# Window-state keys and values loaded from all 128 position blocks: another cut of the state rows into DMA transfers

## The chip, the cores and the metric

The kernel runs on one core of a Trainium2 chip. The metric is the device time of one execution in microseconds; the time of the kernel before is the median of three runs. Views of the profile come from one profiled execution, whose own time stands beside the median below.

## The reference, cut to what matters

One inference step of a decoder layer for 512 prompt tokens and 8 samples with 8 new tokens each. Two attentions run per layer. The change is in the second one for the samples: each new token looks at the last 2048 positions of its sample (the window state, 2048 rows of 8 heads x 64 = 2 KB for keys and as much for values) with three dilations.

```
DIL_PAIRS = ((128, 1), (512, 4), (2048, 16))
def _dilated_attention_sample(q, k_new, v_new, k_buf, v_buf):
    w = k_buf.shape[1]                                  # 2048
    k_all = jnp.concatenate([k_buf, k_new], axis=1)
    v_all = jnp.concatenate([v_buf, v_new], axis=1)
    for window, d in DIL_PAIRS:
        n_k = window // d + 1
        idx = (w + jnp.arange(t))[:, None] - d * jnp.arange(n_k)[None, :]
        kg, vg = k_all[:, idx], v_all[:, idx]
        sc = jnp.einsum('bthd,btjhd->bthj', q, kg) * SCALE
        ...
        parts.append((einsum(e, vg), m, sum(e)))
    o = _combine_branches(parts)
```

The eight new tokens need, of each block of 16 positions, the positions 0 to 7 of all 128 blocks (dilation 16), and the positions 8 to 15 of the last 32 blocks only (dilations 4 and 1). That is 1280 of the 2048 positions.

## The kernel before

The state is viewed as `sk` and `sv`, [sample, p, i, 512]: 128 blocks p, 16 positions i, and 512 floats (2 KB) for a position. So a position lies 2 KB behind the one before it, and a block 32 KB behind the block before it.

Work on past keys and values runs in slots. A slot handles one group q of 512 positions for each of two samples ("pages" of 128 positions, four to a group and sample). Groups q = 0 to 31 come from the paged cache (items 0 to 3, L102 `QUADS`), groups 32 to 43 from the state: items 4 to 7, each two samples, each three groups. The first two groups g = 0, 1 of an item are 64 blocks x positions 0 to 7 (four pages); the third is 32 blocks x positions 8 to 15 (two pages). Keys of group q are handled in slot t = q, its values eight slots later (`LAG`), so the values of the state are used in slots 40 to 51, and from slot 44 (`KSLOTS`) on there are no keys left to do.

Keys: SyncE loads two pages in one DMA into `k_ring` (L832, 512 KB, source made by `state_pair`); VectorE turns them into `kt_sb` (L2271), TensorE scores them (L1296), VectorE adds the mask `lw` and keeps them in `s_sb` (L2308), ScalarE takes the exponentials (L1826). The mask is a host constant that says how often position `keys` is looked at (L79, L81), so it follows whatever order the loads give the positions.

Values: `place_state` (L708) issues eight DMAs a group. For the first two groups each is one quarter of the blocks, 16 blocks x positions 0 to 7: 16 runs of 16 KB at the source, written as 128 rows of 2 KB. For a third group a DMA takes 8 blocks x 8 positions to 64 rows, 128 KB. GpSimd issues those of slots 40 to 43 (all into `v_ring`), SyncE those of slots 44 to 46 and the first halves of 47 to 51, ScalarE the second halves of 47 to 51 between its own work (L1800); after slot 43 the freed `k_ring` and `kt_sb` (as `t_ring`) serve as buffers beside `v_ring`. TensorE turns the probabilities (L1309), ScalarE copies them into `pt_sb` (L1791, for third groups L1795), and TensorE multiplies values by them: L1333 for halves of a group, L1350 for a whole third group. A load into a ring waits until the matmuls of its former content are done (`pv_half`). The order of all this is written out by hand as the sequence of slots t and steps i of each engine's program.

Cache pages (L697, `place_page`) take another form: a page of 128 positions goes to 32 rows of `v_ring`, every fourth, in four pieces of 2 KB a row, so that it is 32 x 4 pieces.

Behind slot 51 the samples' output projection (L1372) and the feed-forward part follow, which need all of it.

Of the kernel before, what the change touches and what calls it, by code (L numbers as in the profile page):

```python
# [15 lines left out]
P = 128  # L16
# [40 lines left out]
def constants():  # L57

    c = np.zeros((P, C_END), np.float32)
    pos = np.concatenate([np.arange(SEQ), PAST + np.arange(NS) % DT]).astype(np.float32)  # L60
    inv = (10000.0 ** (-np.arange(32) / 32)).astype(np.float32)
    ang = (pos[:, None] * inv[None, :]).astype(np.float32).T
    for q in range(4):
        c[32 * q:32 * q + 32, C_COS:C_COS + NT] = np.cos(ang)
        c[32 * q:32 * q + 32, C_SIN:C_SIN + NT] = np.sin(ang) * (1 if q % 2 else -1)
    dist = (SEQ - P) + np.arange(P)[:, None] - np.arange(SEQ)[None, :]
    c[:, C_WMASK:C_WMASK + SEQ] = log_count(dist)
    c[:, C_DMASK:C_DMASK + SEQ] = np.where(dist >= 0, 0, NEG)
    c[:, C_ID:C_ID + P] = np.eye(P)

    p = np.arange(P)
    t, second, b = p % DT, p // 16 % 2, p // DT % 4
    for g in range(3):
        n = 4 if g < 2 else 2
        j, x = np.arange(32 * n) // n, np.arange(32 * n) % n
        if g < 2:
            keys = 16 * (64 * g + 16 * b[:, None] + j // 2) + 4 * (j % 2) + x  # L79
        else:  # L80
            keys = 16 * (96 + 8 * b[:, None] + j // 4) + 8 + 2 * (j % 4) + x  # L81
        c[:, C_LW + P * g:C_LW + P * g + 32 * n] = log_count(WBUF + t[:, None] - keys)
    same = t[:, None] == np.arange(32)[None, :] % DT
    c[:, C_SEL:C_SEL + 32] = same
    c[:, C_SEL + 32:C_SEL + 64] = np.where(same, 0, NEG)

    col = np.arange(MINI_W) - (NS - 2 * DT)
    own = (col[None, :] // DT == second[:, None]) & (col[None, :] >= 0)
    new = t[:, None] - col[None, :] % DT
    c[:, C_MINI:C_MINI + MINI_W] = np.where(own & (new >= 0), 0, NEG)  # L90
    c[:, C_MINI + MINI_W:C_MINI + 2 * MINI_W] = np.where(own, log_count(new), NEG)
    c[:, C_FLAGS] = p % 16 >= DT
    c[:, C_FLAGS + 1] = second == 0
    c[:, C_FLAGS + 2] = second == 1
    c[:, C_FLAGS + 3] = p < 64
    c[:, C_FLAGS + 4] = p >= 64
    return c
# [19 lines left out]
def pages_of(q):  # L117
    it, g = item_of(q)
    return 2 if it >= 4 and g == 2 else 4
# [184 lines left out]
def key_load(q, i):  # L304


    return i | 1 if q >= FIRST[4] else i
# [16 lines left out]
def landings():  # L324


    seen, k_lands, v_lands = [[0] * 8 for sems in range(4)], {}, {}
    for q in range(KSLOTS):
        for i in range(8):
            if i % 4 < pages_of(q):  # L330
                seen[0][i] += key_load(q, i) == i
                k_lands[q, i] = 16 * seen[0][i]
    for q in range(KSLOTS):
        for h in range(2):
            for i in value_loads(q, h):
                s = value_sem(q, i)
                here = seen[sems_of(q + LAG)]
                here[s] += 1
                v_lands[q, s] = 16 * here[s]
    return k_lands, v_lands  # L340
# [56 lines left out]
def build(nc, ins, outs):  # L397
    from contextlib import ExitStack
    ctx = ExitStack()
    with ctx:  # L400
# [299 lines left out]
        def state_rows(state, q, b):  # L700


            it, g = item_of(q)
            if pages_of(q) == 4:
                return state[2 * (it - 4) + b, 64 * g:64 * g + 64, 0:8, :]
            return state[2 * (it - 4) + b, 96:P, 8:16, :]

        def place_state(queue, q, h):  # L708


            ring = ring_of(q + LAG)
            for i in value_loads(q, h):
                s, b = divmod(i, 4)
                rows = slice(0, P) if pages_of(q) == 4 else slice(64 * s, 64 * s + 64)
                src = state_rows(sv, q, s).rearrange("(b a) i c -> b a i c", b=4)[b]
                dst = (k_ring[rows, 4 * h + b, :], v_ring[rows, h, b, :], t_ring[rows, h, b, :])[ring]
                queue.dma_start(dst, src).then_inc(
                    (k_landed, v_landed, t_landed, p_landed)[sems_of(q + LAG)][value_sem(q, i)], 16)
# [23 lines left out]

            return n * 8 + (16 - 8 * par)

        def state_pair(state, q, i):


            n, k = pages_of(q), i % 4
            return state_rows(state, q, i // 4).rearrange("p (s x) c -> p s x c", x=n)[:, :, k - 1:k + 1, :]

        @block.sync
        def _(sp):
# [70 lines left out]
            def load_keys(t, i):  # L823

                if has_k(t) and i % 4 < pages_of(t) and key_load(t, i) == i:
                    if t:
                        last, h = t - 1, i // 4
                        sp.wait_ge(kt_done, PAGE_NO[last, i] + 1 if i % 4 < pages_of(last) else half_end(last, h))
                    if t < FIRST[4]:
                        load_keys_page(t, i)  # L830
                    else:
                        sp.dma_start(k_ring[:, i - 1:i + 1, :], state_pair(sk, t, i)).then_inc(k_landed[i], 16)  # L832

            first_ids = {}

# [1926 lines left out]
```

## Time and profile before

| | |
|---|---|
| median of 3 runs | 1072.36 us (1069.6 to 1074.74) |
| profiled execution, its own time | 1075.88 us |
| its span | 1074.2 us |
| TensorE matmuls busy | 951.3 us, 89% |
| VectorE, ScalarE, GpSimd busy | 667.1, 517.2, 289.1 us |
| DMA | 310.99 MB, mean 290 GB/s |

The span starts 1.7 us short of the execution's own time. TensorE is the busiest engine over the whole, but its share is not even: the part from about 566 to 662 us, where values of the state are used and the prompt's work runs out, is the one with gaps. A view by stretches shows for each the busy time of the engines, the granted TensorE clock as a share of the full one, the share of time in which the DMA engines held packets (two packets in flight make it go slightly over 1) and the GB/s that they moved.

### The profile page before, as it was taken

What the parts mean: (1) busy time and instruction counts of PE and PEld (TensorE: products, weight loads), DVE (VectorE), ACT (ScalarE), POOL (GpSimd) and SP (SyncE); (2) the same over time, 40 slices, a digit from 0 to 9 for tenths busy, and PEclk for the clock granted to TensorE, in tenths of its full rate; (3) what the DMA queues carried; (4) which work ended last, traced back from release to release, by engine and by line L of the source; (5) the groups of instructions that cost most, each with busy time, mean ns of one, the idle gap of its engine ahead of it and who ended that gap; (6) DMA issues with size and microseconds to landing.
All of it is one profiled execution on the core that took longest, in us unless ns stands there. A gap on an engine that the chain in (4) does not pass through costs nothing.

```text
span 1074.2 us, 29350 instructions
## 1 busy us (share of the span) xinstructions
PE 951.3 (89%) x11042; PEld 846.5 (79%) x11042; DVE 667.1 (62%) x1632; ACT 517.2 (48%) x1128; POOL 289.1 (27%) x351
## 2 busy tenths in 40 slices
PE   3989899899977789898996567899999999999996
PEld 3978788788855567676775444899999999999996
DVE  5279745676469978863564254888888888700004
ACT  6554533375226559664332652554555555611114
POOL 1321154545533355335553000000000000133331
PEclk8999999899989989999999688999999999999998
DMA  8799999999999999889998995578687786975642
GB/s 239 256 306 342 328 326 377 355 370 369 382 368 363 355 369 344 303 312 385 378 280 225 239 222 155 209 258 328 235 310 273 266 319 227 336 246 170 219 149 88
DMA packets 158165, 310.99 MB, mean 290 GB/s; under 512 B 13985, under 2 KB 88098, under 8 KB 157026
## 3 DMA queue, kind: packets, MB, share of 16 engines
q1 hardware_dynamic: 133922, 233.92, 63.0%
q0 software_dynamic: 22400, 72.37, 19.2%
q10 hardware_dynamic: 1728, 3.15, 1.2%
q8 instruction: 74, 1.21, 0.5%
q14 instruction: 41, 0.34, 0.1%
HBM read 302.31 MB, written 73.92 MB: 350 GB/s over the span
## 4 chain that ended last, share of the span: by engine, by line
PE 37%; issue 31%; DMA 15%; DVE 7%; ACT 4%; POOL 2%; SPq 2%; POOLq 1%; ACTq 0%; DVEq 0%
PE ps L1468 11%; PE ps L1102 8%; DMA v_ring<-in_cache_v_diff 8%; PE ps L1333 4%; DMA v_ring<-in_state_v_win 4%; PE ps L1296 4%; DMA k_ring<-in_cache_k_diff 3%; DVE kt_sb L2271 2%; PE ps L1253 2%; PE ps L1179 1%; DVE prob L2163 1%; PE ps L1350 1%; PE ps L1163 1%; PE ps L1148 1%; POOL v_ring L697 1%
## 5 line engine op out<-in xcount | busy, mean ns | idle before, releaser
L2271 DVE STREAM_TRANSPOSE kt_sb<-k_ring 128x512 f32<-128x512 f32 x336 | 219.5, 689 | 73.3 <-DMA k_ring<-in_cache_k_diff 35.5
L697 POOL DMA_DIRECT2D v_ring<-in_cache_v_diff x248 | 136.8, 553 | 154.6 <-issue 83.8
L1041 POOL TENSOR_TENSOR c_lo<-c_raw,c_hi 128x1408 fp32r<-128x1408 f32 x14 | 46.7, 3337 | 416.1 <-ACT c_hi L1884 416.1
L1102 PE MATMUL ps<-h_hi,w_hi 128*128 128x288 f32 x384 | 124.2, 323 | 1.9 <-DVE h_lo L2125 1.9
L1102 PE MATMUL ps<-h_lo,w_hi 128*128 128x288 f32 x384 | 115.1, 300 | 0.0
L1102 PE MATMUL ps<-h_hi,w_lo 128*128 128x288 f32 x384 | 114.8, 299 | 0.0
L1333 PE MATMUL ps<-v_ring,pt_sb 128*32 128x128 f32 x2240 | 80.5, 286 | 33.5 <-DMA v_ring<-in_cache_v_diff 21.6
L1296 PE MATMUL ps<-kt_sb,q_st 128*32 128x128 f32 (+1 forms) x2816 | 95.0, 277 | 6.9 <-DVE q_st L2281 4.1
L997 POOL TENSOR_TENSOR w_lo<-w_raw,w_hi 128x1024 fp32r<-128x1024 f32 x24 | 57.3, 2388 | 152.0 <-ACT w_hi L1585 152.0
L1333 PEld LDWEIGHTS ps<-v_ring,pt_sb 128*32 128x32 f32 x2240 | 62.6, 114 | 45.2 <-issue 41.6
L1296 PEld LDWEIGHTS ps<-kt_sb,q_st 128*32 128x32 f32 x2816 | 71.6, 112 | 24.0 <-issue 17.1
L1102 PEld LDWEIGHTS ps<-h_hi,w_hi 128*128 128x128 f32 x384 | 74.0, 193 | 15.7 <-issue 13.5
L1468 PE MATMUL ps<-a_hi,c_hi 128*128 128x288 f32 x352 | 79.1, 296 | 0.2 <-POOL c_lo L1041 0.2
L1401 PE MATMUL ps<-t_h,s_h 128*128 128x288 f32 x264 | 77.9, 295 | 1.2 <-ACT u L1877 1.2
L1468 PE MATMUL ps<-a_lo,c_hi 128*128 128x288 f32 x352 | 78.9, 295 | 0.0
L1468 PE MATMUL ps<-a_hi,c_lo 128*128 128x288 f32 x352 | 78.5, 294 | 0.0
L1401 PE MATMUL ps<-t_l,s_h 128*128 128x288 f32 x264 | 77.9, 295 | 0.0
L1401 PE MATMUL ps<-t_h,s_l 128*128 128x288 f32 x264 | 77.7, 294 | 0.0
L2410 DVE TENSOR_TENSOR s_l<-s_t,s_h 128x512 fp32r<-128x512 f32 x88 | 58.8, 689 | 28.4 <-ACT s_h L1848 18.1
L1102 PEld LDWEIGHTS ps<-h_lo,w_hi 128*128 128x128 f32 x384 | 74.2, 193 | 0.0
L1102 PEld LDWEIGHTS ps<-h_hi,w_lo 128*128 128x128 f32 x384 | 74.0, 193 | 0.0
L2561 DVE TENSOR_TENSOR x<-x,ps 128x512 f32 x7 | 4.8, 689 | 111.1 <-PE ps L1481 111.1
(248 smaller groups left out, 2354.2 us busy)
## 6 DMA issues: line engine op xcount, KB each, us to landing
k_ring<-in_cache_k_diff SPq DMA_DIRECT2D x256, 256.0 KB, 6.8
v_ring<-in_cache_v_diff POOLq DMA_DIRECT2D x248, 256.0 KB, 6.7
out_k_win_sample<-in_state_k_win SPq DMA_DIRECT2D x32, 1020.0 KB, 8.3
out_v_win_sample<-in_state_v_win SPq DMA_DIRECT2D x32, 1020.0 KB, 8.0
k_ring<-in_state_k_win SPq DMA_DIRECT2D x40, 512.0 KB, 7.0
w_raw<-in_w_in SPq DMA_DIRECT2D x24, 512.0 KB, 7.5
g_raw<-in_w_gate SPq DMA_DIRECT2D x11, 1024.0 KB, 5.3
g_raw<-in_w_up SPq DMA_DIRECT2D x11, 1024.0 KB, 5.4
```

The source lines that it names most:

```text
L697: queue.dma_start(dst, src.rearrange("(b j) c -> j b c", b=4))\
L997: nc.gpsimd.tensor_tensor(w_lo[:, n % 3, :], w_raw[:, n % 3, :], w_hi[:, n % 2, :].bitcast(F32), ALU.subtract).then_inc(w_lo_done, 1)
L1041: nc.gpsimd.tensor_tensor(c_lo[j][:, 0:width], c_raw[:, j, 0:width], c_hi[j][:, 0:width].bitcast(F32), ALU.subtract).then_inc(w_lo_done, 1)
L1102: last = nc.tensor.matmul(M[c][:, 0:HALF], wt, act[:, k, c * HALF:(c + 1) * HALF], start=k == 0 and at_first, stop=k == KT - 1 and act is ...
L1148: last = nc.tensor.matmul(M[c][:, 0:n], qT[r, T, qb * P:(qb + 1) * P], kT[r, T, 0:n], start=True, stop=True)
L1253: last = nc.tensor.matmul(M[m % 2], wt, act[:, k, :], start=k == 0 and at_first, stop=k == KT - 1 and act is mix_h and not at_first)
L1296: last = nc.tensor.matmul(S[32 * f:32 * f + 32, c0:c0 + 32 * n], q_st[place_of(it)][:, h, f, r, :], kt_sb[:, 4 * h:4 * h + n, c:c + 32], s ...
L1333: last = nc.tensor.matmul(O[32 * f:32 * f + 32, P * h:P * h + P], pt_sb[:, 4 * f + b, :], values[:, f * P:(f + 1) * P], start=g == 0 and b ...
L1401: last = nc.tensor.matmul(ps[:, bank, 0:HALF], wt[:, k, :], act[:, k, :], start=j in (0, 1, 3) and k == 0 and at_first, stop=k == 3 and wt ...
L1468: last = nc.tensor.matmul(main_ps[:, 2 * bank + c, 0:HALF], wt[j][:, w], a_lo[:, pair, block, :] if low else a_hi[pair][:, block, :], star ...
L2271: V.transpose(kt_sb[:, i, :], k_ring[:, i, :]).then_inc(kt_done, 1)
L2410: V.tensor_tensor(dst[:, :, :], src, high[:, :, :].bitcast(F32), ALU.subtract).then_inc(form_low, 1)
```

## The change

The same positions are read, cut in another way, and the mask constants follow.

```
@@ constants
         if g < 2:
-            keys = 16 * (64 * g + 16 * b[:, None] + j // 2) + 4 * (j % 2) + x
+            keys = 16 * (32 * b[:, None] + j) + 4 * g + x
         else:
-            keys = 16 * (96 + 8 * b[:, None] + j // 4) + 8 + 2 * (j % 4) + x
+            keys = 16 * (96 + 16 * (b[:, None] % 2) + j // 2) + 8 + 4 * (b[:, None] // 2) + 2 * (j % 2) + x
@@ state_rows
             if pages_of(q) == 4:
-                return state[2 * (it - 4) + b, 64 * g:64 * g + 64, 0:8, :]
+                return state[2 * (it - 4) + b, :, 4 * g:4 * g + 4, :]
             return state[2 * (it - 4) + b, 96:P, 8:16, :]
@@ place_state
                 s, b = divmod(i, 4)
-                rows = slice(0, P) if pages_of(q) == 4 else slice(64 * s, 64 * s + 64)
-                src = state_rows(sv, q, s).rearrange("(b a) i c -> b a i c", b=4)[b]
+                if pages_of(q) == 4:
+                    place_page(queue, q, i, state_rows(sv, q, s)[:, b, :])
+                    continue
+                rows = slice(64 * s, 64 * s + 64)
+                src = state_rows(sv, q, s).rearrange("(r a) (u i) c -> u r a i c", r=2, u=2)[b // 2, b % 2]
@@ keys
-        def state_pair(state, q, i):
-            n, k = pages_of(q), i % 4
-            return state_rows(state, q, i // 4).rearrange("p (s x) c -> p s x c", x=n)[:, :, k - 1:k + 1, :]
+        def place_pair(queue, q, i):
+            rows, k = state_rows(sk, q, i // 4), i % 4
+            if pages_of(q) == 4:
+                queue.dma_start(k_ring[:, i - 1:i + 1, :], rows[:, k - 1:k + 1, :]).then_inc(k_landed[i], 16)
+            else:
+                for u in range(2):
+                    src = rows[:, 4 * u:4 * u + 4, :].rearrange("p (s x) c -> p s x c", x=2)
+                    queue.dma_start(k_ring[64 * u:64 * u + 64, i - 1:i + 1, :], src).then_inc(k_landed[i], 16)
```

So a first or second group is now positions 4g to 4g + 3 of all 128 blocks. A DMA of its values is one position of all 128 blocks (256 KB as 128 separate pieces of 2 KB, 32 KB apart at the source), written by `place_page` as a cache page is. A DMA of its keys is two neighbouring positions of 128 blocks (128 pieces of 4 KB). A third group's values go as 16 blocks x 4 positions to a DMA (16 runs of 8 KB), and its keys in two DMAs of half the size instead of one; `landings` counts two arrivals for them.

The instructions of TensorE, VectorE, ScalarE and GpSimd keep kind, number and order; the shapes of the value loads change. In GpSimd's program, at the values of slots 40 to 43, before:

```order
L1018 TENSOR_TENSOR o_lo<-wo_sb,o_hi_64 128x1024
L717 DMA v_ring<-in_state_v_win 128x1x512 x4
L717 DMA v_ring<-in_state_v_win 64x1x512 x8
L717 DMA v_ring<-in_state_v_win 128x1x512 x8
L1068 UNCONDITIONAL_BRANCH
```

and with the change:

```order
L1027 TENSOR_TENSOR o_lo<-wo_sb,o_hi_64 128x1024
L698 DMA v_ring<-in_state_v_win 32x4x512 x4
L721 DMA v_ring<-in_state_v_win 64x1x512 x8
L698 DMA v_ring<-in_state_v_win 32x4x512 x8
L1077 UNCONDITIONAL_BRANCH
```

Nothing moved; the destination of a first or second group's load is 32 rows of four pieces instead of 128 rows of one. In SyncE's program, from the last state keys (one item's third group and all later ones) to the loads behind the last values, before:

```order
L910 DMA g_ffn<-in_norm_ffn_g 128x1024
L832 DMA k_ring<-in_state_k_win 128x1x1024 x16
L717 DMA k_ring<-in_state_v_win 128x1x512 x4
L717 DMA t_ring<-in_state_v_win 128x1x512 x4
L717 DMA k_ring<-in_state_v_win 128x1x512 x4
L717 DMA v_ring<-in_state_v_win 64x1x512 x8
L717 DMA t_ring<-in_state_v_win 128x1x512 x4
L717 DMA k_ring<-in_state_v_win 128x1x512 x4
L803 DMA g_raw<-in_w_gate 128x8x256
L717 DMA v_ring<-in_state_v_win 64x1x512 x8
```

and with the change:

```order
L919 DMA g_ffn<-in_norm_ffn_g 128x1024
L754 DMA k_ring<-in_state_k_win 128x1024 x4
L758 DMA k_ring<-in_state_k_win 64x1x1024 x4
L754 DMA k_ring<-in_state_k_win 128x1024 x8
L758 DMA k_ring<-in_state_k_win 64x1x1024 x4
L698 DMA k_ring<-in_state_v_win 32x4x512 x4
L698 DMA t_ring<-in_state_v_win 32x4x512 x4
L698 DMA k_ring<-in_state_v_win 32x4x512 x4
L721 DMA v_ring<-in_state_v_win 64x1x512 x8
L698 DMA t_ring<-in_state_v_win 32x4x512 x4
L698 DMA k_ring<-in_state_v_win 32x4x512 x4
L812 DMA g_raw<-in_w_gate 128x8x256
L721 DMA v_ring<-in_state_v_win 64x1x512 x8
```

The 16 key loads became 20; the order is the same, and the third groups' value loads keep the destination of 64 rows.

## Rows read from the trace of the kernel before

**Rows 1.** Stretches: us, busy us of the engines (xinstructions), clock, DMA share, GB/s.
```profile
541.00:566.00 25.00, 24.90 (x362) 19.05 (x358) 15.69 (x48) 9.62 (x29) 13.14 (x18) 1.00 0.93 274
566.00:580.00 14.00, 10.25 (x128) 7.49 (x120) 6.46 (x17) 1.79 (x7) 4.49 (x8) 0.88 0.91 223
580.00:618.00 38.00, 21.50 (x408) 17.36 (x408) 11.88 (x54) 20.29 (x45) 4.21 (x8) 0.71 0.99 234
618.00:662.00 44.00, 29.64 (x496) 20.98 (x491) 22.16 (x47) 19.53 (x35) 0.00 (x0) 0.86 0.79 207
662.00:1074.20 412.20, 396.74 (x2969) 391.29 (x2969) 250.28 (x393) 185.03 (x315) 46.71 (x14) 0.99 0.65 239
```

**Rows 2.** Short stretches in which one kind of transfer ran; columns as in rows 1.
```profile
500.00:528.00 28.00, 26.98 (x350) 20.32 (x344) 11.96 (x40) 6.95 (x18) 16.06 (x20) 0.94 1.03 395
552.20:553.80 1.60, 1.60 (x36) 1.13 (x34) 0.71 (x2) 0.70 (x1) 0.00 (x0) 1.00 1.02 392
545.00:550.00 5.00, 5.00 (x57) 3.81 (x51) 3.71 (x9) 0.41 (x3) 4.38 (x5) 1.00 1.00 268
597.00:605.50 8.50, 5.30 (x80) 4.38 (x84) 2.30 (x8) 7.84 (x17) 0.00 (x0) 0.50 1.06 260
571.00:575.00 4.00, 3.96 (x40) 3.11 (x41) 2.61 (x4) 0.00 (x0) 0.01 (x1) 0.66 1.05 193
608.00:612.00 4.00, 1.09 (x8) 0.86 (x8) 1.01 (x6) 3.95 (x12) 0.00 (x0) 1.00 1.07 165
652.50:656.50 4.00, 1.45 (x34) 1.04 (x34) 2.21 (x4) 0.84 (x2) 0.00 (x0) 1.00 0.55 196
```

**Rows 3.** TensorE in order of time: start us, us, work, [idle before <- releaser].
```profile
571.04 1.08 PE L1333 MATMUL ps<-v_ring,pt_sb 128*32 128x128 f32 x32 [2.25 <-DMA v_ring<-in_state_v_win]
...
580.41 2.01 PE L1350 MATMUL ps<-v_ring,pt_sb 128*32 128x128 f32 x64 [1.91 <-DMA v_ring<-in_state_v_win]
...
591.63 1.93 PE L1333 MATMUL ps<-v_ring,pt_sb 128*32 128x128 f32 x32 [5.34 <-DMA v_ring<-in_state_v_win]
...
614.56 3.67 PE L1350 MATMUL ps<-v_ring,pt_sb 128*32 128x128 f32 x64 [5.22 <-DMA v_ring<-in_state_v_win]
...
650.46 1.08 PE L1333 MATMUL ps<-k_ring,pt_sb 128*32 128x128 f32 x32 [1.15 <-DMA k_ring<-in_state_v_win]
653.12 1.08 PE L1333 MATMUL ps<-k_ring,pt_sb 128*32 128x128 f32 x32 [1.57 <-DMA k_ring<-in_state_v_win]
...
657.19 3.33 PE L1350 MATMUL ps<-v_ring,pt_sb 128*32 128x128 f32 x64 [2.62 <-DMA v_ring<-in_state_v_win]
```

**Rows 4.** ScalarE in order of time; the copies of third groups' probabilities.
```profile
578.54 0.84 ACT L1795 ACTIVATE pt_sb<-ps,mini_mask 128x256 f32<-128x256 f32 x2 [12.21 <-PE ps L1309]
...
610.28 0.47 ACT L1795 ACTIVATE pt_sb<-ps,mini_mask 128x256 f32<-128x256 f32 x1
...
654.60 0.84 ACT L1795 ACTIVATE pt_sb<-ps,mini_mask 128x256 f32<-128x256 f32 x2 [2.83 <-PE ps L1309]
```

**Rows 5.** Issues of value loads by GpSimd and SyncE, in order of time.
```profile
566.51 4.49 POOL L717 DMA_DIRECT2D v_ring<-in_state_v_win  x8 [5.65 <-PE ps L1333]
583.01 4.21 POOL L717 DMA_DIRECT2D v_ring<-in_state_v_win  x8 [12.01 <-PE ps L1350]
...
593.62 5.92 SPq L717 DMA_DIRECT2D v_ring<-in_state_v_win  x8
...
641.15 5.11 SPq L717 DMA_DIRECT2D v_ring<-in_state_v_win  x8
```

**Rows 6.** All state value transfers: us from issue to landing.
```profile
DMA to landing us min/median/max: 3.6/8.8/18.5
```

**Rows 7.** State key loads: issue ns min/median/max; SyncE's wait before them, 530 to 664 us.
```profile
L832 SPq DMA_DIRECT2D k_ring<-in_state_k_win x40: 534/535/649, 420.9 to 572.5; - x40
...
SPq L832 <- DVE kt_sb L2271: 39.3, 9, 8.9
```

More of the change, by code:

```diff
@@ L330, in landings @@
             if i % 4 < pages_of(q):
-                seen[0][i] += key_load(q, i) == i
+                if key_load(q, i) == i:
+                    seen[0][i] += 1 if pages_of(q) == 4 else 2
                 k_lands[q, i] = 16 * seen[0][i]
@@ L831, in load_keys @@
                     else:
-                        sp.dma_start(k_ring[:, i - 1:i + 1, :], state_pair(sk, t, i)).then_inc(k_landed[i], 16)
+                        place_pair(sp, t, i)
             first_ids = {}
```

## The prediction

> **What bounds the kernel now.** I read the stretches first [rows 1]. To 566 us TensorE is busy 24.90 of 25.00 us: a faster load gives nothing there. From 662 us on it is busy 396.74 of 412.20 us with work that the change does not touch. Between lie 96 us in which it is busy 10.25 + 21.50 + 29.64 = 61.4 us at a granted clock of 0.88, 0.71 and 0.86, while the DMA engines held packets for 0.91, 0.99 and 0.79 of the time and yet moved only 223, 234 and 207 GB/s. The slots 40 to 51, whose values come from the state, run there. So the gain or loss must be made in 566 to 662 us, and the rate of these loads is the question.
>
> Then the rate by kind of transfer [rows 2], from stretches in which only one kind ran. Cache pages and state keys together: 395 GB/s. State keys alone: 392. State values of first and second groups: 268 issued by GpSimd, 260 by SyncE, the engines full both times. Third groups: 193 with full engines (GpSimd's), 165 where they share the queue with others (SyncE's, from 608), and 196 at a DMA share of 0.55 (from 652.5), which is half of the engines working at full rate and the rest with nothing. The pieces of values have 2 KB on the side of the buffers, as a cache page's have, and the buffers are the same. What is left as a cause is where the pieces lie at the source, and for third groups how many engines get a share.
>
> Last, what this costs on the path: the waits of TensorE for values [rows 3]. They are 2.25, 1.91, 5.34, 5.22, 1.15, 1.57 and 2.62 us, 20.1 in all; an eighth, 2.65 us before 597.64, is not shown, since it lies in the shadow of ScalarE (below).
>
> **First and second groups' values.** 64 DMAs of 256 KB change form, 48 of them issued after 580 us. Number, bytes, order and issuing engines stay. The new source is 128 pieces of 2 KB at a distance of 32 KB, and no trace of before shows just that. Bounds: the slowest row for values of the state, 165 GB/s, and the fastest with pieces of any form, 392 to 395 [rows 2]. I take the upper end, by the row of state keys, which is nearest: they too are 128 separate pieces, come from rows 32 KB apart with the same offsets within the 32 KB for all engines at once, and still ran at 392. The values of before differ from them in that an engine walks one run of 16 KB while its neighbours walk the runs 32 KB beside it, and this form is the slow one.
>
> **Third groups' values.** 32 DMAs of 128 KB: 8 blocks x 8 positions become 16 blocks x 4 positions. The share of 0.55 [rows 2] says that 8 of 16 engines carried SyncE's. With 16 blocks all sixteen have a share. Bounds: still 193 GB/s (all engines full, as GpSimd's at 571) to 392; in between lies 260, since 16 runs beside each other is the form of today's first groups. A group's values are 1.05 MB, thus 2.7 to 5.4 us. More important is that the queue is no longer uneven: the loads behind a third group no longer wait on half the engines.
>
> The Trainium skill says the same of the cause in "DMA: Bandwidth & Descriptors", section "Why a DMA increments its semaphore by 16 and not by 1": the number of engines is the largest up to 16 that divides the slowest dimension of both sides, so 8 for 8 blocks and 16 for 16. The trace agrees with its 0.55. By it the third groups alone would improve, and the rest of the change would be indifferent, which is the first rival's time.
>
> **The path, step by step** (rows 3 to 6; least time from a value load's issue to its landing 3.6 us [rows 6]).
> - Before 582 us: the wait of 2.25 us goes. The next, 1.91 us, was for a third group issued from 566.51 to 571.00 [rows 5]; at 3.6 to 5.4 us it lands by 576.5. ScalarE's copy that L1350 also needs ended at 579.38 [rows 4], so of the 580.41 about 1.0 us is to be had. Together 3.3 us.
> - 591.63: GpSimd starts these loads when L1350 is done, 583.01 [rows 5]. Four issues are half of 4.21, so 585.1, plus 3.6 is 588.7 against 591.5: 2.8 us. The following half's wait (2.65 us) gives nothing more, since ScalarE is busy 7.84 of 8.50 us from 597 on [rows 2] and is next late.
> - 614.56: the loads are issued from 593.62 to 599.54 [rows 5]; they would land by 605 at the latest. ScalarE's copy of the probabilities ends at 610.75 [rows 4], so L1350 starts about 610.9: 3.7 us.
> - 618 to 646: no wait for values; ScalarE, VectorE and TensorE hand each other work. 0.
> - 650.46 and 653.12: 1.15 + 1.57 = 2.7 us. 657.19: the copy ends at 655.44 [rows 4], L1350 at 655.6: 1.6 us. The loads for it, issued 641.15 to 646.26 [rows 5], land by 650.
>
> Sum 3.3 + 2.8 + 3.7 + 2.7 + 1.6 = 14.1 us. From 580 to 657 us some 18 MB of loads pass (48 x 0.26 + 3 x 1.05 + 2.1 of weights); at 392 GB/s that is 46 us, well inside the shortened stretch. I take 13, because a shift passes between engines with an order of their own and not one to one. What is late next is ScalarE.
>
> **Keys.** First and second groups: 32 DMAs of 128 pieces of 4 KB as before, now two positions of 128 blocks instead of four of 64. Cost 0 if the rate stays at 392, which I take, since piece, distance and engines stay. At 268 [rows 2], 16.8 MB would take 63 us instead of 43, partly under TensorE's work before 566. Third groups: 8 more DMAs at 535 ns of SyncE are 4.3 us in four places, hidden by the 39.3 us for which SyncE waits before such loads [rows 7]. Without that cover each pair would delay the next keys by 1 us. The mask is data only: 0.
>
> **The sum.** Against the profiled execution's own time, 1075.9 - 13 = 1062.9 us. The median of the runs is 3.5 us below that execution, so 1059.4 on its scale; I say 1060.
>
> **Rivals.**
> - Only the balance of the third groups improves, the first groups stay at 260. Then 1.0 + 0 + 3.7 + 0.5 + 1.6 = 6.8 us: by 599.5 us 6.3 MB are on their way from 582 at 260, landing at 606, still ahead of ScalarE. 1065.5 us.
> - The change does not do what it says: rates stay as they are, because neither number of engines nor position of the pieces sets them but the total of what is queued. Then 0 to -3 us, 1071. For it: with full engines GpSimd's third groups had 193 GB/s. Against it: the DMA share of 0.55 and the 392 of the keys in the same stage.
> - Slower: the new value loads collide at the memory. All 128 pieces of a DMA have the same offset within 32 KB, an engine's next piece is 1 MB further (32 blocks), and four such loads follow each other. If this gives the third groups' rate, 48 x 0.262 = 12.6 MB after 580 take 65 us at 193 GB/s instead of 48 at 260, and 76 at 165: 17 to 28 us more, against some 9 us of idle DMA time between 618 and 662 (0.21 x 44) that can take it up. So +8 to +19 us, 1080 to 1091. It decides from about 230 GB/s down. For it: two forms at this spacing are already slow, which the trace doesn't explain. Against it: the keys. The Trainium skill has a rule in this direction in "DMA: Bandwidth & Descriptors", section "Latency and other measured facts": full rate up to a row pitch of 512 KB and half of it at 4 MB, with 32 KB not among the pitches named. Today's slow loads at 32 KB are not explained by it.
>
> **How the numbers follow.** Fast as forecast 0.50, balance only 0.16, no effect 0.12, collision (of values, or of keys) 0.22. A measurement of this kernel can tell about 0.5%, 5.4 us, from no change. The forecast and most of the second case are faster; part of the second and the third are the same. So faster 0.64, same 0.14, slower 0.22. The range runs from 1052 (the whole sum, with the clock of 0.71 in the stage recovering and matmuls there faster by some us) to 1084, which takes in the lower half of the collision.
>
> **What would show it.** Right: in the stage of values a rate of 350 GB/s or more where only first groups' loads run, no DMA share near 0.55 with third groups' loads, TensorE's waits for state values under 5 us in sum, ScalarE as the releaser of L1333 and L1350, and the stage from 566 to 662 us some 13 us shorter at a higher clock, with the stretch behind it unchanged at 412 us. Wrong: rates of 260 or below for L1333's buffers, or state keys under 350 GB/s between 420 and 570 us. If the rates rise and the time doesn't fall, then the path through ScalarE was longer than read.

## The result and the profile after

The changed kernel took 1067.99 us (median of 20 runs, 1060.8 to 1074.06) against 1075.26 us of the kernel before (20 runs beside it, 1067.52 to 1080.36). The ratio is 0.9934, interval 0.9911 to 0.9957; by this ratio 7.1 us less. Forecast were 12.4 us less (1072.4 to 1060), a ratio of 0.988. So the sign was right and the gain little more than half of what was said. The profiled execution has a span of 1070.0 us, before 1074.2.

For the comparison I cut both traces at the same events instead of at fixed times: the **key stage** runs from the first load of state keys to the first load of state values, the **value stage** from there to the load of the sample rows that the output projection needs. Kernel before; columns as in [rows 1]:

```profile
420.89:541.37 120.48, 108.25 (x1638) 84.46 (x1638) 73.56 (x251) 68.19 (x201) 56.35 (x83) 0.97 0.94 340
541.37:661.93 120.56, 85.92 (x1376) 64.56 (x1374) 56.19 (x164) 51.09 (x113) 21.84 (x34) 0.84 0.90 231
```

The changed kernel:

```profile
417.35:545.30 127.95, 110.10 (x1638) 85.33 (x1638) 73.92 (x251) 68.09 (x201) 56.25 (x82) 0.96 0.98 321
545.30:658.20 112.90, 84.84 (x1376) 63.11 (x1374) 56.11 (x164) 50.97 (x113) 21.84 (x34) 0.85 0.80 245
```

But for one of GpSimd's, the same numbers of instructions ran in each. The value stage is 7.7 us shorter and its DMA share fell from 0.90 to 0.80. But the key stage, where the prediction set 0, is 7.5 us **longer**, at a higher DMA share and a lower rate (321 for 340 GB/s). In these two executions the two cancel, and most of the difference in span is the start of the key stage, 3.5 us earlier and behind work that the change doesn't touch. That start lay anywhere from 415.2 to 421.5 us in the executions profiled for this study, so one trace is not good to 7 us in the time of an event, while the length of a stage is steadier. The times of many runs decide, and the experiments are judged by both.

What the loads did, changed kernel, stretches in which one kind prevailed, same columns:

```profile
594.00:598.00 4.00, 2.51 (x68) 1.89 (x60) 2.85 (x20) 1.71 (x5) 0.00 (x0) 0.91 1.04 391
...
598.60:603.50 4.90, 0.45 (x12) 0.42 (x16) 1.60 (x3) 4.84 (x11) 0.00 (x0) 0.80 1.06 214
...
548.80:553.00 4.20, 4.20 (x58) 3.06 (x47) 2.91 (x8) 0.54 (x3) 4.17 (x5) 1.00 0.87 265
573.00:577.00 4.00, 4.00 (x40) 2.93 (x36) 2.95 (x10) 0.00 (x0) 1.33 (x3) 1.00 1.06 227
```

First and second groups' values reach 391 GB/s when SyncE issues them (594), for 260 in [rows 2]. GpSimd's first ones (548.8) move 265 at a share of 0.87; why the engines are not full there, I can't say. Third groups stay slow although all engines now work: 214 (SyncE's, 598.6) and 227 (GpSimd's, 573), where [rows 2] had 165 and 193.

The state keys, changed kernel: a stretch with first groups' keys, cache pages and two weight loads, and one with a third group's keys and cache pages:

```profile
503.00:523.00 20.00, 18.52 (x258) 14.16 (x259) 10.80 (x38) 4.42 (x8) 10.32 (x15) 1.00 1.02 391
...
528.00:540.00 12.00, 8.38 (x116) 6.34 (x114) 4.03 (x13) 2.21 (x5) 5.08 (x9) 0.86 1.02 236
```

First groups' keys are as fast as ever. Behind a third group's keys the full engines move 236 GB/s. Who pays for it is in the waits of TensorE over the key stage (us in total, times, longest). Before:

```profile
PE ps L1333 <- DMA v_ring<-in_cache_v_diff: 5.1, 3, 3.3
```

and with the change:

```profile
PE ps L1342 <- DMA v_ring<-in_cache_v_diff: 11.3, 8, 3.8
```

The cache pages' values, which GpSimd loads for other slots, come late: 6.2 us more of waiting. TensorE's own waits in this stage name no key load.

The waits of TensorE in the value stage, changed kernel, 541 to 662 us, summed by releaser (L1342, L1359, L1373, L1800, L1804, L1817 are the former L1333, L1350, L1364, L1791, L1795, L1808):

```profile
PE ps L1342 <- ACT pt_sb L1800: 11.8, 4, 5.9
PE ps L1359 <- ACT pt_sb L1804: 5.4, 3, 3.1
PE ps L1342 <- DMA v_ring<-in_state_v_win: 4.3, 2, 3.7
PE ps L1373 <- ACT ptm L1817: 4.2, 3, 3.5
PE ps L1359 <- DMA v_ring<-in_state_v_win: 2.2, 1, 2.2
```

and single ones, TensorE in order of time with columns as in [rows 3]:

```profile
580.42 3.19 PE L1359 MATMUL ps<-v_ring,pt_sb 128*32 128x128 f32 x64 [2.18 <-DMA v_ring<-in_state_v_win]
...
591.52 1.94 PE L1342 MATMUL ps<-v_ring,pt_sb 128*32 128x128 f32 x32 [3.66 <-DMA v_ring<-in_state_v_win]
...
603.05 3.64 PE L1342 MATMUL ps<-k_ring,pt_sb 128*32 128x128 f32 x64 [5.88 <-ACT pt_sb L1800]
...
611.06 2.02 PE L1359 MATMUL ps<-v_ring,pt_sb 128*32 128x128 f32 x64 [1.44 <-ACT pt_sb L1804]
...
624.03 1.93 PE L1342 MATMUL ps<-t_ring,pt_sb 128*32 128x128 f32 x32 [4.05 <-ACT pt_sb L1800]
...
654.88 2.02 PE L1359 MATMUL ps<-v_ring,pt_sb 128*32 128x128 f32 x64 [0.93 <-ACT pt_sb L1804]
```

Of 22.7 us of waits for state values (10.2 and 9.8 for `v_ring`, 2.7 for `k_ring`) 6.5 are left; ScalarE's copies are the releasers of most others. The waits for loads at 614.56, 650.46, 653.12 and 657.19 of [rows 3] are gone; the two between 576 and 592 are not.

One difference in this stage is no load. The same hundred or so matmuls, a whole third group and the output projection behind it (L1372, now L1381), run almost without a wait in both kernels. First before, from 637.70, then with the change, from 636.60; columns as in [rows 1]:

```profile
637.70:646.40 8.70, 8.34 (x105) 4.95 (x106) 5.95 (x15) 2.65 (x5) 0.00 (x0) 0.84 1.02 270
636.60:648.00 11.40, 11.04 (x101) 5.94 (x101) 6.02 (x15) 2.54 (x5) 0.00 (x0) 0.59 0.79 255
```

The mean granted clock of TensorE was 0.84 and then 0.59, and the stretch took 2.7 us longer. So the length of a stage in one trace also carries the clock of that execution.

### The profile page after: what moved, and what is told of

Its sections match the earlier page's. It is cut to its first block, busy times and chain, and to the rows that moved or that the text cites. A ratio compares the mean times of both kernels' runs of the same rounds, so it can differ in the third digit from the quotient of the medians.

```text
span 1070.0 us, 29358 instructions
## 1 busy us (share of the span) xinstructions
PE 948.3 (89%) x11042; PEld 844.3 (79%) x11042; DVE 667.0 (62%) x1632; ACT 516.6 (48%) x1128; POOL 287.7 (27%) x351
## 4 chain that ended last, share of the span: by engine, by line
PE 38%; issue 32%; DMA 15%; DVE 6%; ACT 5%; POOL 2%; POOLq 1%; ACTq 0%; SPq 0%; DVEq 0%
DMA v_ring<-in_cache_v_diff 12%; PE ps L1477 11%; PE ps L1111 9%; PE ps L1342 5%; PE ps L1305 4%; PE ps L1262 2%; DVE kt_sb L2280 1%; DMA v_ring<-in_state_v_win 1%; ACT rot L1616 1%; POOL v_ring L698 1%; PE ps L1318 1%; PE ps L1359 1%; PE ps L1188 1%; DMA x<-in_x_prompt 1%; DMA k_ring<-in_cache_k_diff 1%
## 5 line engine op out<-in xcount | busy, mean ns | idle before, releaser
L1342 PE MATMUL ps<-v_ring,pt_sb 128*32 128x128 f32 x2240 | 79.2, 283 | 40.8 <-DMA v_ring<-in_cache_v_diff 34.0
L1342 PEld LDWEIGHTS ps<-v_ring,pt_sb 128*32 128x32 f32 x2240 | 61.1, 113 | 53.2 <-issue 49.5
```

What stands on the lines that cost most here:

```text
L1342: last = nc.tensor.matmul(O[32 * f:32 * f + 32, P * h:P * h + P], pt_sb[:, 4 * f + b, :], values[:, f * P:(f + 1) * P], start=g == 0 and b ...
```

## The experiments

Medians of before beside them were 1074.29 us (a), 1073.12 (b) and 1071.48 (c). All ratios are against the kernel before; "key" and "value" are the two stages, from one profiled execution. The edits are shown cut to what matters; the counts of landings follow them. In runs with keys or values in another order the positions no longer match the mask, while the amount of work stays.

| | key us | value us | ratio, interval |
|---|---|---|---|
| before | 120.5 | 120.6 | 1 |
| changed | 128.0 | 112.9 | 0.9934 (0.9911 to 0.9957) |
| a1 new values only | 122.0 | 110.7 | 0.9879 (0.9835 to 0.9923) |
| a2 new keys only | 129.1 | 122.7 | 1.0065 (1.0035 to 1.0095) |
| a3 third keys in one DMA | 121.1 | 111.7 | 0.9883 (0.9837 to 0.993) |
| a4 third groups as before | 121.0 | 107.1 | 0.9874 (0.983 to 0.9917) |
| b1 first keys in halves of rows | 142.2 | 115.9 | 1.0193 (1.0145 to 1.024) |
| b2 third keys to 128 rows, 2 DMAs | 121.8 | 112.9 | 0.9885 (0.9835 to 0.9935) |
| b3 first values cut as 16 x 8 | 122.5 | 122.4 | 0.9986 (0.9962 to 1.001) |
| b4 a4 with the halves in turn | 121.7 | 107.3 | 0.9894 (0.9826 to 0.9962) |
| c1 a4 with a quarter of the bytes | 120.4 | 102.9 | 0.9853 (0.9802 to 0.9903) |
| c2 a3 with the halves in turn | 120.9 | 105.7 | 0.9889 (0.9857 to 0.9921) |
| c3 b4 again | 120.5 | 109.0 | 0.9905 (0.9874 to 0.9936) |

### Which part loses: a1 to a4

a1 takes the old form of all state keys back, a2 the old form of all state values:

```
a1  place_pair(queue, q, i):
-    (the new form, two DMAs for third groups)
+    src = old_state_rows(sk, q, i // 4).rearrange("p (s x) c -> p s x c", x=n)[:, :, k - 1:k + 1, :]
+    queue.dma_start(k_ring[:, i - 1:i + 1, :], src).then_inc(k_landed[i], 16)
a2  place_state(...):
-    (the new form)
+    src = old_state_rows(sv, q, s).rearrange("(b a) i c -> b a i c", b=4)[b]
```

> Values as changed, keys of all state groups loaded as before; the two no longer hold the same positions, so the sample outputs mean nothing, the work is the same. In the two traces the way from the first state key load to the last matmul of the first state-independent item grew from 120 to 127.5 us with the changed keys, and the way from there to 662 us fell from 122 to 114. Theory K (the keys' new form gives back half of what the values gain): ratio to the kernel before 0.985 to 0.989, DMA rate between 525 and 540 us back near 390 GB/s. Rival V (the values gain only the 0.66% measured, the key stage's 7 us are chance of one execution): 0.992 to 0.995.

> Keys as changed, values of all state groups loaded as before (positions do not match, sample outputs mean nothing). Theory K: slower than before by 4 to 8 us, 1.004 to 1.007, with key packets of about 300 ns in the stretches of the third groups' keys. Rival V: 1.000 within 0.2%.

Measured 0.9879 and 1.0065. In us of the 1074.29: the new values alone give 13.0, the new keys alone cost 7.0, together 6.0 against the 7.1 measured for both. The two parts add up, as far as intervals of 8.3 to 17.7 and 3.8 to 10.2 us can say. The prediction's total for values (13) agrees with the first; its 0 for keys was wrong by about 7.

a3 leaves everything as changed and only puts the keys of third groups back into one DMA:

```
-                for u in range(2):
-                    src = rows[:, 4 * u:4 * u + 4, :].rearrange("p (s x) c -> p s x c", x=2)
-                    queue.dma_start(k_ring[64 * u:64 * u + 64, i - 1:i + 1, :], src).then_inc(k_landed[i], 16)
+                src = rows.rearrange("p (s x) c -> p s x c", x=2)
+                queue.dma_start(k_ring[:, i - 1:i + 1, :], src).then_inc(k_landed[i], 16)
```

> As changed, but each third group's keys come in one DMA to 128 rows as before instead of two to 64 rows each (positions of third groups do not match, sample outputs mean nothing). If the keys' loss is the third groups' alone, this equals the run with all keys as before (0.985 to 0.989) and no stretch of 300 ns key packets is left. If the first groups' keys (two positions of all 128 blocks) share in it, it lies between that run and the changed kernel's 0.993.

0.9883, the same as a1 within the intervals, with the key stage at 121.1 us and TensorE's waits for cache pages' values at 5.9 us, where the changed kernel had 11.3. So all of the loss comes from the eight key loads of third groups that became sixteen, and the first groups' new keys cost nothing, as forecast. Number, size and destination rows of those loads change together here; b1 and b2 part them.

a4 is a3 with third groups' values and mask as before too, so that only first and second groups are changed:

```
-                src = state_rows(sv, q, s).rearrange("(r a) (u i) c -> u r a i c", r=2, u=2)[b // 2, b % 2]
+                src = state_rows(sv, q, s).rearrange("(b a) i c -> b a i c", b=4)[b]
```

> First and second groups as changed, third groups (keys, values, mask) as before; computes the reference. Against the run above it lacks only the 16 blocks x 4 positions form of third groups' values. My term for the balance of the queues says that this form is worth 2 to 4 us: 0.988 to 0.992 here. If the balance is worth nothing, it equals the run above.

0.9874. I had expected to lose the 2 to 4 us of the balance. By the times no loss can be seen, and the value stage is not longer but shorter (107.1 for 111.7). Most of that difference is the clock: the hundred matmuls named above, in a3 and in a4,

```profile
632.70:644.10 11.40, 11.03 (x105) 5.96 (x106) 6.04 (x15) 2.53 (x5) 0.00 (x0) 0.60 0.77 249
625.00:632.30 7.30, 6.92 (x101) 3.72 (x101) 6.05 (x15) 2.40 (x5) 0.00 (x0) 1.00 0.89 305
```

account for 4.1 of the 4.6 us, and this clock doesn't follow the form of the loads: with the old form in a2 it was 0.60 there, with the new one in c2 1.00. Why the balance brought nothing is seen in the rates; a4, SyncE's first groups and its third group:

```profile
586.00:590.00 4.00, 2.62 (x36) 2.23 (x36) 1.60 (x9) 2.65 (x7) 0.00 (x0) 0.50 1.02 378
594.00:598.00 4.00, 3.97 (x66) 3.34 (x58) 1.34 (x3) 3.95 (x7) 0.00 (x0) 0.70 0.99 203
```

Here a third group runs among other loads, 203 GB/s with full engines. Alone, the old form moved 196 GB/s with a share of 0.55 [rows 2]; the new one moves 214 to 227 with a share of 1.06. So the new form keeps all the engines busy for little more than the rate that half of them reach, and the loads behind it find none free. The step "with 16 blocks all sixteen have a share" fits the share of 1.06, and was worth nothing that the times show.

### Why 64 rows are slow: b1 to b4

By now two theories stood against each other. **Source side** (the prediction's): the rate hangs on how the pieces lie in memory. **Write side**: a DMA that writes 64 neighbouring rows of the buffer reaches only about half of the ways into it, and one in which each engine writes 8 neighbouring rows also uses them badly, whatever is read. Which engine writes which rows no trace shows; here and below it is read from the shapes, a cut of 16 x 8 being taken as 8 rows for each of 16 engines. The write side explains the new third keys (64 rows each), the third values in either form (64 rows), the old first values (128 rows, but cut as 16 runs x 8 rows), and the fast ones: cache pages and the new first values, which `place_page` puts on every fourth row of all 128.

b1 makes a fast transfer slow, if the write side is right: it is a4 with each first group's key DMA cut into rows 0 to 63 and 64 to 127. Pieces and places at the source stay.

```
-                queue.dma_start(k_ring[:, i - 1:i + 1, :], rows[:, k - 1:k + 1, :]).then_inc(k_landed[i], 16)
+                for u in range(2):
+                    half = slice(64 * u, 64 * u + 64)
+                    queue.dma_start(k_ring[half, i - 1:i + 1, :], rows[half, k - 1:k + 1, :]).then_inc(k_landed[i], 16)
```

> Base: first and second groups changed, third groups as before (0.9874; 121 us from the first state key load to the first state value load, 107 from there to the load of the sample rows). The only edit: each first and second group's key DMA (128 blocks to 128 rows of the buffer) is issued as two, blocks and rows 0 to 63 and 64 to 127. Source pieces, their order and all positions stay. Theory W (the rate is set on the side of the buffer: a DMA that writes 64 neighbouring rows gets about half of the write paths, some 220 GB/s, whatever it reads): the key stage grows from 121 to 130 us or more, key packets of 4 KB at 270 to 340 ns, ratio 0.995 to 1.01. Rival S (source addresses of the third groups set it): 4 KB packets at 165 to 190 ns as in the base, key stage within 3 us of it, 0.986 to 0.991.

Measured 1.0193, the slowest kernel of the study, and a key stage of 142.2 us for 121. b1 over the key stage, and near its end:

```profile
419.16:561.39 142.23, 114.55 (x1638) 88.37 (x1638) 73.99 (x251) 67.97 (x201) 56.21 (x83) 0.92 1.03 287
...
534.00:548.00 14.00, 12.51 (x138) 9.43 (x136) 3.18 (x5) 4.00 (x11) 6.80 (x9) 0.94 1.04 274
```

The engines are full throughout (1.03) and move 287 GB/s, where 340 had left them 6% free. The size of the effect was underestimated by the write-side expectation too.

b2 is the reverse: still two DMAs of 256 KB for a third group's pair of keys, but each writes all 128 rows, 2 KB a row.

```
-                    src = rows[:, 4 * u:4 * u + 4, :].rearrange("p (s x) c -> p s x c", x=2)
-                    queue.dma_start(k_ring[64 * u:64 * u + 64, i - 1:i + 1, :], src).then_inc(k_landed[i], 16)
+                    queue.dma_start(k_ring[:, i - 1 + u, :], rows[:, 4 * u:4 * u + 4, :]).then_inc(k_landed[i], 16)
```

> The changed kernel with one edit: a third group's keys still come in two DMAs that read the same 32 blocks x 4 positions each, but write 128 rows of 2 KB instead of 64 rows of 4 KB (so the positions do not match, sample outputs mean nothing). Theory W: the third groups' key stretches run at 350 to 390 GB/s, the key stage is back at 120 to 122 us from 128, ratio 0.986 to 0.990. Theory S: same source, same slow stretches, 127 to 129 us and 0.993.

0.9885 and a key stage of 121.8 us: the loss is gone with as many DMAs and smaller pieces. So it is not the number of DMAs, nor SyncE's time to issue them. b2 over the stage, and behind a third group's keys:

```profile
415.26:537.10 121.84, 108.53 (x1638) 84.83 (x1638) 73.77 (x251) 68.14 (x201) 56.17 (x83) 0.97 0.95 338
522.00:527.00 5.00, 4.00 (x79) 3.08 (x73) 1.72 (x10) 0.00 (x0) 2.21 (x4) 1.00 1.02 367
```

b3 is a4 with the new source of first groups' values (one position of all blocks, pieces 32 KB apart), but dealt out as 16 x 8, so that 8 neighbouring rows belong together, as before the change:

```
-                    place_page(queue, q, i, state_rows(sv, q, s)[:, b, :])
+                    src = state_rows(sv, q, s)[:, b, :].rearrange("(e a) c -> a e c", e=8)
+                    dst = (k_ring[:, 4 * s + b, :], v_ring[:, s, b, :], t_ring[:, s, b, :])[ring]
```

> Base as in the first run of this call. The only edit: a first or second group's value DMA still reads one position of all 128 blocks, but in an order of 16 x 8 that the two sides cannot merge, to 128 rows, so that each of the 16 engines writes eight neighbouring rows of 2 KB as the kernel before did (positions do not match, sample outputs mean nothing). Theory W: back to the rate of before, 260 GB/s and 2 KB packets of about 130 ns where only these loads run, stage of the values 116 to 122 us instead of 107, ratio 0.995 to 1.002. Theory S: 85 to 90 ns packets as in the base, 107 us, 0.987.

0.9986: the whole gain of the change is gone, although each DMA reads the same 128 pieces. b3, SyncE's first groups:

```profile
596.00:602.00 6.00, 2.54 (x36) 1.79 (x36) 2.30 (x7) 5.20 (x10) 0.00 (x0) 0.63 1.05 257
```

257 GB/s are the 260 of [rows 2]. So where the pieces of a DMA lie at the source does not set its rate, and the prediction's cause is out: a run of 16 KB and pieces 32 KB apart are equally slow when written as 16 x 8, and b1 slows a transfer with its source untouched. What b3 does not isolate is why 16 x 8 is slow. Its edit changes the order of the pieces too: within one of the 16 parts they now lie 16 blocks (512 KB) apart, with `place_page` 32 blocks (1 MB). And 8 neighbouring rows for an engine can't be all of it: the old state keys, 64 blocks x 2 rows of 4 KB, would by equal shares also give each engine 8 neighbouring rows, and ran at 392 GB/s [rows 2].

The Trainium skill has the rule for 64 rows in "SBUF — State Buffer", section "Door 1: The DMA port swizzle (why `[64,N]` ≈ `[32,N]`)": which of 16 ports a row is written through hangs on bits of its number, and 64 neighbouring rows reach only 8 of them. The runs agree: 192 to 227 GB/s for 64 rows, 391 for 128. Cited before the change, this rule would have spoken against cutting the third keys. It does not by itself give the 257 GB/s of b3, whose 128 rows reach all ports; that the engines of a 16 x 8 DMA meet at the same ones is my reading, and no run shows a port.

b4 tries to write both halves of the rows at once. Third groups' value loads go in the order 0 to 3 (rows 0 to 63), then 4 to 7 (rows 64 to 127). b4 is a4 with the halves in turn, so that two loads in flight write to different halves:

```
 value_loads
-    return range(8) if h == 0 else ()
+    return (0, 4, 1, 5, 2, 6, 3, 7) if h == 0 else ()
```

> Base as in the first run of this call, computes the reference. The only edit: the eight value DMAs of a third group are issued alternately for the two samples (rows 0 to 63, rows 64 to 127, rows 0 to 63, ...) instead of four and four. Theory W: where GpSimd issues them (its DMAs use eight engines each, in turns), both halves of the rows are written at once and the 4 KB packets fall from 340 ns towards 170, the DMA rate there from 193 to 300 GB/s or more; SyncE's stay at 8 engines and about 190 to 200 GB/s. Time about as the base, 0.985 to 0.988, since one wait of 2 to 3 us hangs on them. Theory S: packets stay at 320 ns or more.

It works in part. GpSimd's third group in a4, same columns:

```profile
564.00:568.00 4.00, 4.00 (x44) 2.93 (x35) 2.89 (x10) 0.00 (x0) 1.72 (x4) 1.00 1.06 192
```

and in b4:

```profile
567.00:571.00 4.00, 4.00 (x67) 3.36 (x58) 3.34 (x12) 0.00 (x0) 2.78 (x6) 1.00 0.90 247
```

192 became 247 GB/s at a lower DMA share; the expectation of 300 and more was missed, and SyncE's third groups alone did not change (190 GB/s at a share of 0.51, from 613 to 616 us). The value stage stayed at 107.3 us and the ratio at 0.9894.

### What is left in the value stage: c1 to c3

c1 asks how much faster loads could still give. It is a4 with 128 of the 512 floats of each state value piece loaded and used (the matmuls read the same 128 each time, their number and size are unchanged):

```
-                    place_page(queue, q, i, state_rows(sv, q, s)[:, b, :])
+                    dst = (k_ring[b:P:4, 4 * s:4 * s + 4, 0:P], v_ring[b:P:4, s, :, 0:P], t_ring[b:P:4, s, :, 0:P])[ring]
+                    queue.dma_start(dst, state_rows(sv, q, s)[:, b, 0:P].rearrange("(b j) c -> j b c", b=4)).then_inc(
     ... (third groups' loads and the matmuls' operand likewise)
```

> Base: first and second groups changed, third groups as before (0.9874, value stage 107 us). The edit: each state value DMA moves the first 128 of 512 floats of every piece, and the matmuls of the state's values all read those (so the samples' window output is left wrong; number of DMAs, pieces, waits and matmuls stay, bytes of state values are a quarter). It shows the floor of the value stage. Theory A (after the change the path through ScalarE, with its issues and table loads, and the order of the slots bounds the stage): 101 to 107 us, at most 6 less than the base, ratio 0.982 to 0.988. Rival D (the stage is still bound by the bytes): 95 us or less, 0.976 or less.

0.9853, and a value stage of 102.9 us with the DMA engines at 0.39. TensorE's waits in it:

```profile
PE ps L1342 <- ACT pt_sb L1800: 13.0, 4, 6.5
PE ps L1359 <- ACT pt_sb L1804: 6.4, 4, 3.1
PE ps L1373 <- ACT ptm L1817: 3.1, 3, 2.4
PE ps L1342 <- DMA v_ring<-in_state_v_win: 1.2, 2, 0.9
```

So what is late next is ScalarE, as the prediction said, and the floor of this stage with its present order is about 103 us: 17.6 us under before by the trace, 15.8 us by the times. Of that the new first groups' values alone take 13 or so. So little room is left between a1, a3, a4, b2, b4 and c2, and their intervals overlap.

c2 puts the halves in turn on the new form of third groups (a3 with the order of b4):

> The changed kernel with its third groups' keys in one DMA (0.9883, value stage 111.7 us), and third groups' values (16 blocks x 4 positions, 16 engines) issued alternately for the two samples. With the old form (8 blocks x 8 positions, 8 engines) the value stage was 107.1 us. Theory W: all 16 engines of a new-form DMA sit on the same half of the rows at once (220 GB/s) and hold up what is queued behind; issued alternately the halves overlap little, as each engine takes its DMAs in order, so the rate rises less than for eight-engine DMAs: 2 KB packets 110 to 150 ns, value stage 109 to 111 us. If it is 107 or less, alternation repairs the new form too. Positions do not match for third groups, sample outputs mean nothing.

Stage 105.7 us, ratio 0.9889: a miss, since I had expected 109 to 111 us and little help for a form that occupies all sixteen engines. Of the 6.0 us to a3, though, 4.1 are the clock again (the hundred matmuls in 7.3 us at 1.00), and the remaining 1.9 are hardly more than two profiles of one kernel can differ by (1.7, see c3). Its SyncE third group ran at

```profile
594.00:599.00 5.00, 0.94 (x17) 0.76 (x20) 1.60 (x3) 4.94 (x12) 0.00 (x0) 0.84 1.06 270
```

against the 214 GB/s with the order of the changed kernel. The rate is what speaks for the write side: with all engines on either load, two loads in turn write all 128 rows.

c3 is b4 run again in five rounds:

> The same kernel as the one with alternating samples (first and second groups changed, third groups in the form of before, their values issued alternately): it computes the reference. Repeated to narrow its ratio to the kernel before, 0.9894 [0.983, 0.996] so far. I expect 0.986 to 0.989, below the changed kernel's 0.9934, and value stage 107 us, key stage 121 us.

0.9905, a little above the expected 0.986 to 0.989, with a value stage of 109.0 us for 107.3 in b4. So two profiles of one kernel differ by 1.7 us in this stage.

d1 is the kernel before once more, to see how far the 0 net change of the two stages can be chance:

> The kernel before once more, for a second profile. By timed runs the changed kernel gains 7.1 us (0.66%), in the two profiles the key and the value stage together are 241.0 us before and 240.9 after, and only the start of the key stage differs, by 3.5 us. If the first profile of before had short stages by chance, this one shows 243 to 247 us for the two together. If it shows 240 to 242, the gain of the timed runs lies elsewhere and stays open.

Key stage 120.9, value stage 122.0, together 242.9 for the 241.0 of the first profile and the 240.9 of the changed kernel; begin of the key stage at 420.6 (420.9). This lies between what the two theories expected, so it decides little: 2 us of the 7.1 are explained by a short first profile. Some 3 us more come from which executions were profiled: the changed kernel's took 1071.72 us, 3.7 above the median of its runs, the one of before 1075.88 us, 0.6 above. For the same reason a3 (7.0 us above its median) and a4 (5.0 below) can't be compared closely by their stages. The start of the key stage varies among kernels that don't touch what lies before it (421.0 in a1, 421.5 in a3, 415.2 in a4). In which stage the rest lies can't be placed from single traces and stays open.

## Why the prediction was partly right

**What bounds the kernel, and where.** Right. The gain was made in the value stage, and the part behind 662 us (412.2 us before) takes 411.8 with the change. To 566 us, though, I took TensorE's 24.90 of 25.00 busy us [rows 1] for the whole story: "a faster load gives nothing there" is true, but a slower one still loses, because the 94% of DMA share in the key stage left 7 us of 120 free.

**First and second groups' values.** The rate is right (391 for the 392 taken), the reason wrong. "What is left as a cause is where the pieces lie at the source" was reached by elimination, and the list left out the rows that are written: "the pieces of values have 2 KB on the side of the buffers, as a cache page's have, and the buffers are the same" compares the size and the tile, and not which rows each engine writes. The fact stood in the order of instructions, 32x4x512 against 128x1x512. b3 shows that the gain goes with this cut; the order of the pieces, which changes with it, is not parted from it.

**Third groups' values.** Measured 214 to 227 GB/s, near the lower end (193) of the range. "More important is that the queue is no longer uneven" failed: a4 without this part is as fast by its times (0.9874 to 0.9883 of a3). The share of 0.55 with 196 GB/s [rows 2] was read as "half of the engines working at full rate"; but all the engines on the same 64 rows got no more than 227, so the rows were the limit and not the engines.

**The path.** 14.1 us, taken as 13. By the times new values alone give 13.0 us (a1). In the stage they give 9.8 (a1), 8.9 (a3), 7.7 (with the change) and 13.5 (a4), so the total is right within a wide margin. By steps it is less right. Counted from the first load of state values (541.37 before, 545.30 with the change), the changed kernel is ahead, at places named by their times before,

- by 3.9 us at the whole third group of 580.41, where 3.3 were forecast, although it still waits 2.18 us for its load (39.0 us behind the first load before, 35.1 now);
- by 4.0 us at 591.63: the 2.8 us of this step came to 0.1, since GpSimd's load took 5.5 us from its fourth issue to its landing (585.85 to 591.38), not the 3.6 of the shortest;
- by 7.4 us at 614.56: 3.4 for the 3.7 of the forecast;
- by only 2.3 us behind the output projection (646.37 before, 648.01 now). This stretch was set at 0 and lost 5.1: 2.7 by the lower clock shown above, most of the rest in waiting for ScalarE (4.05 us before 624.03, 2.79 at that place before);
- by 7.7 us at the end: 5.4 for the 4.3 of the last steps.

ScalarE took the part of late releaser (5.88 us before 603.05), as said.

**Keys, the failed step.** First and second groups: 0, right (a3). Third groups: "8 more DMAs at 535 ns of SyncE are 4.3 us in four places, hidden" priced the issue and not the transfer. Both halves were given a destination of 64 rows, by the diff itself, while the text on third groups' values had the rate for 64 rows at hand, 193 to 196 GB/s [rows 2]. The four places cost 7.0 us by the times (a2), and the key stage, which holds three of them, is 7.5 us longer. With the rate of those rows the term could be estimated: a third group's keys are 1.05 MB, 5.4 us at 196 GB/s instead of 2.7 at 392. Three of the four groups are loaded in the key stage, thus 8 us more of full engines there, against 7 us that the engines had free and that lie elsewhere in the stage. What is not covered delays the cache pages in GpSimd's queue, for which TensorE waits 6.2 us longer.

**The rivals.** "Only the balance improves" is the reverse of what happened. "No effect" is ruled out by the 391 GB/s. The collision did not come about for values; a collision of keys was named in its chance and in the sentence "state keys under 350 GB/s between 420 and 570 us", and that sign did show: 236 GB/s at 528 to 540 us. Its mechanism (equal offsets at the memory) was wrong: b1 brings the slowness about with the offsets untouched.

**The number.** 1072.4 - 13.0 (values) + 7.0 (third keys) = 1066.4 us; measured 0.9934 x 1072.4 = 1065.3. So the error of the forecast is the key term, as far as the intervals tell; that the 13 of the values came out so well, with steps of it off by 2.7 and 5.1 us, is in part luck. The kernels that avoid it (a3, a4, b2) gain 12.3 to 13.5 us and, at 0.9874 to 0.9885, beat the changed kernel by some 5 us or more; a4, with the least change, is what I would keep.

## What to carry to other kernels

When a load is slow, compare how its pieces are dealt out over the rows that it writes before looking for a cause at the source; test it by reading the same pieces into the rows in another cut. Cutting one DMA of 128 rows into two of 64 is no neutral step: price the transfer, not only the issue, and look for those who share its engines. When the DMA engines are nearly full, a stage bound by TensorE has no slack for slower transfers, though faster ones give it nothing. And before a few us between the stages of two traces are put down to a load, compare how long the same matmuls took in both.

## What the runs showed of the hardware

- A DMA that writes 64 neighbouring rows runs at about half the rate of one that writes 128: 192 (cut as 8 blocks x 8 positions, a4) to 227 GB/s (16 x 4, changed kernel) against 391, with full engines each time. Cutting the 32 key loads of first and second groups (16.8 MB) in this way made the whole kernel 3.2% slower than its neighbour (b1 1.0193, a4 0.9874).
- A DMA to 128 rows cut as 16 x 8 rows of 2 KB: 257 (b3) and 260 GB/s (before), whether it reads runs of 16 KB or pieces 32 KB apart. Cut as 64 x 2 rows of 4 KB: 392 (keys before).
- 128 pieces of 2 KB at 32 KB distance, with steps of 1 MB inside a DMA, read at 391 GB/s: no loss at the source.
- Two loads to opposite halves of the rows in turn: 247 for 192 GB/s (GpSimd's, 8 x 8, b4 and a4), 270 for 214 (SyncE's, 16 x 4, c2 and changed kernel).
- The same hundred or so matmuls took 7.3 us at a granted clock of 1.00 (a4) and 11.4 us at 0.60 (a3).
